# Three feed-forwards of a fused two-block kernel: one 512-column stretch by seven block products in place of eight

## The reference, cut to what matters

```python
def swiglu(h, w_in, w_out):
    g, u = split_cols(h @ w_in, (D_FF, D_FF))
    return (jax.nn.silu(g) * u) @ w_out
...
x = x + 0.5 * swiglu(rms_norm(x, g[4]), ffn2_w_in[layer], ffn2_w_out[layer])
```

## Time and profile before

| | us |
|---|---|
| median of three executions | 1623.52 |
| the profiled execution | 1622.07 |
| its span, first to last instruction | 1620.7 |
| TensorE busy in it | 1595.9 |
| DVE busy | 1111.8 |
| ACT busy | 861.7 |
| POOL busy | 202.5 |

### The profile page before, as it was taken

The page is one execution under the profiler, slowest core; times in us unless marked ns, Lnnn a source line. Parts: engine busy times, 40 slices in busy tenths (PEclk is TensorE's granted clock), DMA queues, the critical chain, the costliest instruction groups (busy, mean ns, idle before and its releaser), DMA issues.

```text
span 1620.7 us, 21120 instructions
## 1 busy us (share of the span) xinstructions
PE 1595.9 (98%) x8050; PEld 1331.6 (82%) x8050; DVE 1111.8 (69%) x1769; ACT 861.7 (53%) x1324; POOL 202.5 (12%) x267
## 2 busy tenths in 40 slices
PE   8999999999999999999999999999999999999998
PEld 6888887788888888888889888888889877888886
DVE  6765888867655556555596775655568997776566
ACT  5554556755654545444555555544454457454444
POOL 2498401000000000000000000000014442100000
PEclk9999999999999999999999999999999999999999
DMA  9766756444466565666654553555575554556553
GB/s 283 236 212 212 237 144 193 152 140 153 143 185 191 184 189 175 193 184 192 208 172 157 164 183 114 184 183 190 187 261 170 161 157 143 182 195 191 190 186 110
DMA packets 187542, 295.21 MB, mean 182 GB/s; under 512 B 13510, under 2 KB 108144, under 8 KB 186160
## 3 DMA queue, kind: packets, MB, share of 16 engines
q1 hardware_dynamic: 183264, 275.93, 54.4%
q0 software_dynamic: 3888, 17.60, 3.4%
q10 hardware_dynamic: 288, 0.33, 0.1%
HBM read 288.29 MB, written 5.25 MB: 181 GB/s over the span
## 4 chain that ended last, share of the span: by engine, by line
PE 85%; DVE 9%; ACT 4%; issue 2%; POOL 1%; DMA 0%; SPq 0%; DVEq 0%; ACTq 0%
PE b L446 24%; PE b L448 24%; PE b L447 24%; PE b L668 4%; DVE wlo L1678 3%; PE b L670 2%; ACT whi L1119 2%; PE b L691 1%; PE b L921 1%; PE b L903 1%; PE b L512 1%; PE b L528 1%; PE b L612 1%; PE b L565 1%; ACT R L1208 1%
## 5 line engine op out<-in xcount | busy, mean ns | idle before, releaser
L1678 DVE TENSOR_TENSOR wlo<-raw,whi 128x1024 fp32r<-128x1024 f32 (+1 forms) x523 | 653.1, 1251 | 428.2 <-ACT whi L1119 427.0
L1119 ACT ACTIVATE whi<-raw 128x1024 fp32r<-128x1024 f32 (+1 forms) x523 | 549.7, 1053 | 557.0 <-PE b L448 520.1
L446 PE MATMUL b<-whi,hT 128*128 128x512 f32 (+1 forms) x1040 | 413.0, 397 | 10.0 <-DVE wlo L1678 8.5
L448 PE MATMUL b<-whi,hT 128*128 128x512 f32 (+1 forms) x1040 | 405.1, 390 | 0.0
L447 PE MATMUL b<-wlo,hT 128*128 128x512 f32 (+1 forms) x1040 | 404.6, 389 | 0.0
L446 PE MATMUL b<-whi,oT 128*128 128x512 f32 x672 | 265.2, 395 | 0.3 <-DVE oT L1769 0.3
L448 PE MATMUL b<-whi,oT 128*128 128x512 f32 x672 | 262.0, 390 | 0.0
L447 PE MATMUL b<-wlo,oT 128*128 128x512 f32 x672 | 261.6, 389 | 0.0
L446 PEld LDWEIGHTS b<-whi,hT 128*128 128x128 f32 x1040 | 195.9, 188 | 55.5 <-DVE wlo L1678 10.5
L448 PEld LDWEIGHTS b<-whi,hT 128*128 128x128 f32 x1040 | 195.8, 188 | 41.6
L447 PEld LDWEIGHTS b<-wlo,hT 128*128 128x128 f32 x1040 | 196.2, 189 | 37.7
(11 more groups left out here) (349 smaller groups left out, 1828.3 us busy)
## 6 DMA issues: line engine op xcount, KB each, us to landing
raw<-in_ffn_w_in SPq DMA_DIRECT2D x350, 256.0 KB, 3.1
raw<-in_ffn_w_out SPq DMA_DIRECT2D x88, 512.0 KB, 3.3
raw<-in_w_ff SPq DMA_DIRECT2D x64, 512.0 KB, 4.1
raw<-in_w_in SPq DMA_DIRECT2D x36, 512.0 KB, 3.7
raw<-in_x_w_kv SPq DMA_DIRECT2D x32, 512.0 KB, 4.3
raw<-in_even_w_in SPq DMA_DIRECT2D x24, 512.0 KB, 4.1
raw<-in_odd_w_in SPq DMA_DIRECT2D x24, 512.0 KB, 4.1
raw<-in_x_w_q SPq DMA_DIRECT2D x16, 512.0 KB, 3.9
```

The source lines that it names most:

```text
L446: T.matmul(out, ah, bh, start=start, stop=False, skip_group_check=skip)
L448: return T.matmul(out, al, bh, start=False, stop=stop, skip_group_check=skip)
L1119: E.activation(K.whi[j % NSPLIT][:, 0:n], K.raw[j % NRAW][:, 0:n], ACT.Copy).then_inc(*S.whi.done(j))
L1678: V.tensor_tensor(K.wlo[j % NSPLIT][:, 0:n], K.raw[j % NRAW][:, 0:n], K.whi[j % NSPLIT][:, 0:n].bitcast(F32), ALU.subtract).then_inc(*S.wl ...
```

## The change

In chunks 6 and 7 of each of f1, f2 and f3 the product of the 256 x 1024 activations with 1024 x 1024 of `w_in` (512 gate and 512 up columns) is computed as one `block`. Rows, inner dimension and columns are each cut in two, which gives activations A11 to A22 and weights B11 to B22 (B.1 up, B.2 gate columns), and the eight products of these become seven, P1 to P7 in `PRODUCTS`, each of four 128-row steps (two pieces of six matmuls, 84 matmuls in all for 96):

- Four products need sums of weights: T1 = B11 + B12, T2 = T1 + B22, T3 = B22 + B12, T4 = T2 + B21. They are made by DMA. SP loads B11, B11 and B22 into six 512 KB tiles in R1 (`tile_load`), the first 26 pieces before the block and one with each ring piece; POOL starts DMAs that add the other quadrants to them (`block_sums`, `accum_op=ALU.add`): eight before the block, and two that turn T2 into T4 inside it, once DVE has read T2's two pieces.
- Four need sums of activations. DVE makes them in chunk 1 (`activation_sums`), ACT and DVE split them in chunk 2 (`row_sums`), into mT. That buffer held split rows of `mem` for a later layer; this splitting moves from f1's chunks 5 and 6 to f2's chunks 9 and 10.
- The seven products run in banks 4, 5 and 6. P1's value is copied out by ACT (`snapped`) before P2 is added to its bank; P6, P5, P7, P3 and P4 are combined by five additions of DVE (`joined`: U2, V, G1, G0, U1). ACT applies silu and DVE multiplies, 512 columns at once.
- A piece of the block is used up after 6 matmuls, not 12, and there are 14 of them for the 8 before. Chunk 5's two down pieces stand after P7 and after P3; those of chunks 6 and 7 are done in chunk 8.

```diff
+PRODUCTS = (("P1", 4, 1, "B11"), ("P6", 5, 1, "T2"), ("P5", 6, 1, "T1"), ("P2", 4, 0, "B21"), ("P7", 5, 0, "T3"),
+            ("P3", 6, 0, "B22"), ("P4", 5, 0, "T4"))
+TILE_LEAD = 26
...
@@ pe_program, ffn @@
+        def block(c):
...
+            for q, (name, bank, opens, of) in enumerate(PRODUCTS):
+                if name == "P2":
+                    pe.wait_ge(*S.snapped.at(key))
+                elif name == "P7":
+                    pe.wait_ge(*S.joined.at((*key, "U2")))
+                elif name == "P3":
+                    pe.wait_ge(*S.joined.at((*key, "V")))
+                elif name == "P4":
+                    pe.wait_ge(*S.joined.at((*key, "G1")))
+                else:
+                    open_bank(bank)
...
+                for h in range(2):
...
+                    pe.wait_ge(*S.wlo.at(j))
+                    hi, lo = K.split_views(j)
+                    for kk in range(2):
+                        ins = products(banks[bank][:, :], K.factor(name, 2 * h + kk), (hi[:, kk, :], lo[:, kk, :]),
+                                       bool(opens) and h == kk == 0, h == kk == 1, True)
...
+            free[4] = (S.product.at((f.name, c, 0)),)
+            free[5] = (S.joined.at((*key, "U1")),)
@@ act_program, ffn, block @@
+            behind(1)
+            act.wait_ge(*S.dense.at((*key, "P1")))
+            act.wait_ge(*S.product.at((f.name, c - 1, 1)))
+            E.activation(K.fs[0], banks[4][:, :], ACT.Copy).then_inc(*S.snapped.done(key))
+            behind(9)
+            opened(1, "G1")
+            behind(11)
+            opened(0, "G0")
@@ dve_program, ffn, block and activation_sums @@
+            reached(3)
+            dve.wait_ge(*S.snapped.at(key))
+            joined("U2", "P6", 5, K.fs[0], K.fs[2])
+            reached(5)
+            joined("V", "P5", 6, K.fs[0], K.fs[1])
+            reached(9)
+            dve.wait_ge(*S.joined.at((*key, "V")))
+            joined("G1", "P7", 5, K.fs[1], K.fs[1])
+            reached(11)
+            dve.wait_ge(*S.joined.at((*key, "U2")))
+            joined("G0", "P3", 6, K.fs[2], K.fs[2])
+            reached(12)
+            dve.wait_ge(*S.dense.at((*key, "P2")))
+            gated(0, banks[4][:, :])
+            reached(13)
+            joined("U1", "P4", 5, K.fs[0], K.fs[0])
+            dve.wait_ge(*S.joined.latest())
+            gated(1, K.fs[0])
...
+                V.tensor_tensor(rows[:, 0, :, :], A22, A21, ALU.subtract).then_inc(*S.dve_own.done())
...
+                V.scalar_tensor_tensor(out=rows[:, 1, :, :], in0=rows[:, 0, :, :], scalar=-1.0, in1=A11,
+                                       op0=ALU.mult, op1=ALU.subtract).then_inc(*S.row_summed.done((f.name, 0)))
@@ pool_program, block_sums @@
+            for name, total in (("T1", "T1"), ("T2", None), ("T3", "T3")):
+                for h in range(2):
+                    add(name, "B12", h, S.tiled[f.slot(c, name, h)].at((*key, name)), total)
+            for h in range(2):
+                add("T2", "B22", h, S.tile_sum[f.slot(c, "T2", h)].at((*key, "T2B12")), "T2")
+            for h in range(2):
+                add("T4", "B21", h, S.wlo.at(K.at[b, 2 + h]), "T4")
@@ sp_program @@
+        while tiles and K.at[f"{tiles[0][0].name}b{tiles[0][1]}", 0] - TILE_LEAD + tiles[0][2] <= j:
+            tile_load(*tiles.pop(0))
```

More of the change, by code:

```diff
@@ L136, in __init__ @@
         S.x_turned = tuple(s[f"xt{i}"] for i in range(5))
+        S.tiled = tuple(s[f"tile{i}"] for i in range(8))
+        S.tile_sum = tuple(s[f"sum{i}"] for i in range(8))
         S.masks, S.cst, S.columns, S.mem_turned, S.sm, S.bl, S.mem, S.rel, S.cl, S.gf, S.cum, S.dec = (
@@ L143, in __init__ @@
         S.out = (s["out0"], s["out1"], s["out2"])
-        self.plan, self.first, self.at, self.place = [], {}, {}, {}
+        self.plan, self.source, self.rings, self.first, self.at, self.place = [], [], [], {}, {}, {}
         self.stats, self.stat_n = {}, 0
@@ L168, in memory @@
         self.xv = R2[:, 2048:4096].rearrange("p (t n) -> p t n", t=2)
+        self.tile = [R1[:, 1024 * i:1024 * i + 1024] for i in range(8)]
         self.vsb = sb("vsb", [P, 2, 512])
@@ L247, in gain, with operand, activation, factor @@
         return self.gcol[:, i:i + 1]
+    def operand(self, j):
+        kind, of, i = self.source[j]
+        return self.raw[of % NRAW] if kind == "ring" else self.tile[i]
+    def activation(self, f, c, t):
+        c0 = f.begin(c)
+        return self.fa[(2 * c0 + t) % 4][:, 256 * (c - c0):256 * (c - c0) + 256]
+    def factor(self, name, kt):
+        if name in ("P1", "P2", "P4"):
+            k, t = kt + 4 * (name != "P1"), int(name == "P4")
+            return tuple(a[:, k, P * t:P * t + P] for a in self.hT)
+        at = 512 * ("P5", "P6", "P7", "P3").index(name) + P * kt
+        return tuple(a[:, :, :].rearrange("p k t -> p (k t)")[:, at:at + P] for a in self.mT)
     def split_views(self, j):
@@ L438, in piece @@
         j = len(K.plan)
+        K.source.append(("ring", len(K.rings), None))
+        K.rings.append(j)
         K.plan.append((name, l, k0, nk, tuple(cols)))
@@ L723, in ffn @@
         last, groups = f.nch - 1, range(f.per // 2)
-        for c in range(f.nch):
+        for c in f.units():
+            if c in f.blocks:
+                block(c)
+                continue
             if c:
-                beside = {2 if f.before is None and c == 1 else 0: lambda: turn(c - 1)}
+                beside = {n: lambda p=p: turn(p) for n, p in enumerate(f.ahead_of(c))}
+                if f.before is None and c == 1:
+                    beside = {2: lambda: turn(0)}
                 if f.before is None and c == 1:
@@ L1115, in weights @@
             n = K.plan[j][3] * sum(w for _, w in K.plan[j][4])
-            act.wait_ge(*S.loaded[j % NRAW].at(j))
+            kind, of, i = K.source[j]
+            if kind == "ring":
+                act.wait_ge(*S.loaded[of % NRAW].at(j))
+            else:
+                act.wait_ge(*S.tile_sum[i].at(of))
             if j >= NSPLIT:
                 act.wait_ge(*S.dense.at(("w", j - NSPLIT)))
-            E.activation(K.whi[j % NSPLIT][:, 0:n], K.raw[j % NRAW][:, 0:n], ACT.Copy).then_inc(*S.whi.done(j))
+            E.activation(K.whi[j % NSPLIT][:, 0:n], K.operand(j)[:, 0:n], ACT.Copy).then_inc(*S.whi.done(j))
     def pieces(name, n=None):
@@ L1260, in ffn @@
                     silus(0)
-                if c and p == (3 if f.before is None and c == 1 else 1):
-                    high(c - 1)
+                for n, chunk in enumerate(f.ahead_of(c)):
+                    if p == (3 if f.before is None and c == 1 else 1 + n):
+                        high(chunk)
+                if f.blocks and c == 2 and p in (0, 1):
+                    row_sums(p)
                 if c == 0 and p == 1 and f.before:
@@ L1677, in weights @@
             dve.wait_ge(*S.whi.at(j))
[L1678 removed]
+            V.tensor_tensor(K.wlo[j % NSPLIT][:, 0:n], K.operand(j)[:, 0:n], K.whi[j % NSPLIT][:, 0:n].bitcast(F32),
                             ALU.subtract).then_inc(*S.wlo.done(j))
@@ L1980, in ffn @@
         last, groups = f.nch - 1, f.per // 2
-        for c in range(f.nch):
+        for c in f.units():
+            if c in f.blocks:
+                block(c)
+                continue
             for p in pieces(f"{f.name}up{c}"):
-                if c and p == (3 if f.before is None and c == 1 else 1):
-                    low(c - 1)
+                for n, chunk in enumerate(f.ahead_of(c)):
+                    if p == (3 if f.before is None and c == 1 else 1 + n):
+                        low(chunk)
+                if f.blocks and c == 1:
+                    activation_sums(p)
+                if f.blocks and c == 2 and p in (1, 2):
+                    row_sums(p - 1)
                 if c == 0 and p == 1 and f.before:
@@ L2868, in x_turned, with tile_load @@
                     ).then_inc(*S.x_turned[i].done(0, step=16))
-    for j, (name, l, k0, nk, cols) in enumerate(K.plan):
+    blocks, holder = [(f, c) for f in FFNS for c in f.blocks], {}
+    tiles = [(f, c, i) for f, c in blocks for i in range(6)]
+    def tile_load(f, c, i):
+        (name, of), h = TILES[i // 2], i % 2
+        slot = f.slot(c, name, h)
+        old, holder[slot] = holder.get(slot), f"{f.name}b{c}"
+        if f.before != "f1":
+            sp.wait_ge(*S.turned.at(("o", f"{f.before}1", 1)))
+        if old:
+            sp.wait_ge(*S.wlo.at(K.at[old, {"T1": 4, "T3": 8, "T2": 12}[name] + h]))
+        k0, c0 = f.quadrant(c, of, h)
+        Q.dma_start(K.tile[slot].rearrange("p (k n) -> p k n", k=2),
+                    D[f.w_in][f.l, k0 * P:(k0 + 2) * P, c0:c0 + 512].rearrange("(k p) n -> p k n", p=P)
+                    ).then_inc(*S.tiled[slot].done((f.name, c, name), step=16))
+    for n, j in enumerate(K.rings):
+        name, l, k0, nk, cols = K.plan[j]
+        while tiles and K.at[f"{tiles[0][0].name}b{tiles[0][1]}", 0] - TILE_LEAD + tiles[0][2] <= j:
```

(7 more changed lines are left out.)

142 lines of the change are left out of this document (124 added, 18 removed).

## The result

The changed kernel takes 1647.6 us (median of 4 runs, 1646.5 to 1653.1) where the kernel before, in the same comparison, takes 1623.2 us (1621.6 to 1624.6). The ratio is 1.0157, with a 95% interval of 1.0146 to 1.0169: 24.4 us slower, outside the range of the prediction, and at the price that rival A gave at its full end (1648). The profiled execution took 1647.6 us, its span 1646.3.

What follows compares the result with a forecast made beforehand. TensorE, busy 98%, was taken to bound the kernel: -8.2 us for 36 matmuls, +7.4 block waits, +1.0 activation sums, 0 for DMA, +0.2 in all, giving 1623.7 us; 8-in-10 range 1618 to 1641.

Steps and rivals of the forecast that it cites:

- rival A: f1's, f2's and f3's chunks 2 and 3: ring starves, whi waits for loads; 1636, or 1648 at full price; chance 0.30.
- DMA part: Ring loads before each block: an addition costs a plain load, queue 10 us behind, lead 10.8 us, so 0 us of wait.
- point of decision: Ring starves once an addition costs TensorE's queue more than 1.6 us, only 0.1 over the plain load.
- The sum by its rule: Additions at twice a plain load: 6 us a piece, 19 behind, 8.2 us wait in each of three, 25 us.
- restart of 0.11 us after a wait: TensorE after any wait: second matmul starts 0.34 and not 0.227 us after the first, 0.11 more each time.
- The block's sum: Each block: 12 matmuls fewer; waits of 0.7 us inside and 1.8 at its end, 2.5 a block, 7.4 in three.
- The sums on DVE: Activation sums in chunk 1: its down piece waits 0.22 us for bank 0, restart 0.11, in each of three: 1.0 us.
- The split of mem: Moved from f1's chunks 5 and 6 to f2's 9 and 10, hidden by the loop's 2.8 us to spare: 0.
- the two late additions: Turn T2 into T4 inside the block, needed some 16 us later; slowest POOL load took 10.4 us: 0.
- Rival B: Block waits smaller because wlo and PSUM reads overlap more; 1 us of waits left a block, 1619; chance 0.16.
- rival C: Other small stalls: POOL's DMA issue stretches DVE, or additions inside the block are late; 1627 to 1633; chance 0.08.

Runs made afterwards that it cites:

- the block alone: Changed kernel without the block's tile loads and POOL's adding copies, its products running on whatever the tiles hold: 1625.5 us, 1.0012 of the kernel before.

## Why the prediction was wrong

**The step that failed** is in its DMA part: "I take the plain load, because it is the nearest row". The row was near in queue and size, but not in what is done: an addition took 2.9 us of the DMA engines and not 1.5, measured on thirty of them and against thirty plain loads in the same places. Its count was short as well: the sum gave each of six pieces one addition, but eight come before the block. The prediction had put the point of decision 0.1 us over the plain price, and the other end of the bound, twice the price, gave 19 us behind and 8.2 us of wait a block. Measured: 8 to 10 us a feed-forward lost between chunk 0 and chunk 3. So the mechanism, the place, and the dear end of the price were in the text; the choice between the ends, and the chance of 0.30, were not what a margin of 0.1 us allows. Between two ends of which one lies on the edge of a threshold and the other far beyond, the forecast belongs beyond it.

The range's top, 1641, was the second fault, from the same place: it left out the dearer half of A although nothing in the trace spoke against twice the price.

The Trainium skill, "Collectives: The Full Stack", Part 3, on the two source reads that halve the rate of an add in the DMA engine, was weighed and set aside. The packets agree with it: 176 ns against 84. The sum by its rule, 25 us, is also about what the kernel lost, but that the sizes meet is partly luck: that sum had six additions and no slow matmuls in it, and the real loss is 18 us of waits for wlo, 5 of slow matmuls and 2 in chunk 1. HBM was read for one source only (310.31 MB on the page of the changed kernel, 285.14 in the block alone: 25.2 MB for 48 transfers of 524,288 bytes, once each), so no second read of HBM is behind the price. That it is the read of the tile in SBUF is likely, but no row shows it.

**A claim in rival A** was too mild as well: that half of the additions trail and the loss is 12 us in all. They did trail, and that held the loss under what the density alone gives; but the wait came with slow matmuls behind it. In the three feed-forwards TensorE waited 5.5, 6.9 and 5.5 us for wlo and lost another 1.5, 1.7 and 1.5 us at the lower clock. The prediction's restart of 0.11 us after a wait held for the block's short waits (0.31 or 0.34 us to the second matmul); after the longest wait of each feed-forward the second came after 0.34 us in f1 and f3 and 0.59 in f2, and the slow ones followed.

**The block's sum** was right. Predicted from the end of chunk 5's ups to the end of chunk 8's: 44.7 us; by the multiplications that follow them, 532.2 to 577.0, it is 44.8. Predicted waits at chunk 8's start 0.57 and 0.97, measured as starts late by 0.66 and 0.87 (each without its slow second matmul); P2's first piece 0.29, measured 0.33; P7's and P5's next to nothing. So 96 matmuls less 12 gave 2.7 us a block and the waits took about 2.6 back (67.0 us for 67.1), where 2.5 was worked out; the block alone has the same waits (0.30, 0.67 and 0.88 in f1).

**The sums on DVE** were sized too small. The down piece of chunk 1 waited 0.8 us in f1 and in f3 where 0.22 was expected, since DVE reached the multiplication 1.6 us after the down piece's start and not 1.05. In f2 it reached it after 0.98 us, and the wait was 0.15, near the expectation. Moving the sums gave 2.2 us in three feed-forwards (1619.9 to 1617.7, in one comparison), which is these three waits and their restarts. With them, +0.2 becomes about +1.3, within what the block alone measured (0.5 to 3.4 over).

**Zero terms.** The split of mem and the two late additions cost nothing: the two landed after 6.9 and 8.1 us, under the 10.4 taken as their bound, and P4 waits for none of them. Rival B's smaller waits were not there, nor rival C's, though POOL's issue of an addition takes 1.26 us against 0.71 for a plain transfer of the same bytes (means of thirty). The count in the prediction, 7014 to 6978, should read 8050 to 8014; the difference is right.

## What to carry to other kernels

An accumulating DMA like this one (HBM into SBUF, float32, 2 KB packets) is to be costed at twice the plain load of its bytes, and then against the time in which it must fit: what decides is the work of all queues in a stretch against the stretch and the lead of the stream beside it, not the mean share of the DMA engines. The cure costs nothing where there is room in time: the same bytes, one per four pieces, took the loss away. A product scheme that trades matmuls for additions pays where those additions' reads fall at its end; a piece of unrelated work put behind the last product, and the operand sums put where nobody waits, turned +24 us into -5.

## What the runs showed of the hardware that I had not expected

- A 2 KB packet of an addition into SBUF took 176 ns, a plain one on SP's queue 84 ns; at 1 KB an adding packet took 101 ns, more than half of 176, so that the same bytes cost more in smaller packets.
- While both queues had work they moved nearly one packet for one (785 and 782, 317 and 329, 991 and 991), whatever the packets' sizes. So in f1 the ring got 84 GB/s beside adding packets of 2 KB, 88 beside plain ones of 4 KB and 120 beside adding ones of 1 KB, against the 188 that it needs.
- After each of the changed kernel's longest waits (TensorE idle 3.7 us and more) eight or nine matmuls ran 0.42 us apart, at a granted clock of 0.59 over f1's stretch (0.51 from 475.8 to 479.2 us, which is the lower level), then 0.227 again. In the kernel with one tile per two pieces, whose longest waits kept TensorE from starting for 2.3 to 3.4 us, no such stretch followed. With the half-width additions one came after 2.9 us and none after 3.0, and after 3.7 us three matmuls ran at full pace before it, so the length of the wait alone does not tell.
